# One 512-column matmul for the high weight block in three projections, with the two halves added by VectorE

## The reference, cut to what matters

```
q    = xt @ w_pq                      # layer 1, 2048 x 2048, then q . sub_k1, q . sub_k2, top-k, experts
xBC  = proj[:, 4096:10240]            # layer 2, h @ in_w, 6144 of its columns
xBC  = silu(causal_depthwise_conv(xBC, conv_w, conv_b))   # 4 taps along the tokens
k, v = split(x @ kv_w, 2, axis=-1)    # layer 3, k is 2048 x 3072
```

## Time and profile before

| | |
|---|---|
| time, median of 3 (us) | 3421.45 (3420.68 to 3424.72) |
| span of the profiled execution (us) | 3418.1 |
| PE, DVE, ACT, POOL busy | 95%, 70%, 47%, 19% |
| chain that ended last: PE, DVE, issue, ACT | 83%, 5%, 3%, 3% |

### The profile page before, as it was taken

How to read it: one execution, slowest core, us unless ns; L and a number is a source line. 1 busy time by engine, 2 the same in 40 slices (tenths; PEclk the granted TensorE clock), 3 DMA queues, 4 the chain that set the end, 5 groups by cost and what they waited for, 6 DMA issues and landing times.

```text
span 3418.1 us, 64505 instructions
## 1 busy us (share of the span) xinstructions
PE 3259.0 (95%) x21980; PEld 2977.2 (87%) x21980; DVE 2395.3 (70%) x3845; ACT 1602.5 (47%) x2243; POOL 661.4 (19%) x635
## 2 busy tenths in 40 slices
PE   7999999999999999999999989999999999999997
PEld 7787899999889998899777879998888779987996
DVE  6675459189778987799898776335888877554455
ACT  4654446533454344433344555545665444444442
POOL 1000029800111001100000116885221111100000
PEclk9999999999999999999999999999999999999998
DMA  6434544666787668866555874666665886765443
GB/s 195 148 99 140 162 148 153 186 203 212 235 264 225 211 211 258 263 201 213 167 172 177 265 245 123 185 190 191 208 208 172 272 267 220 248 194 177 136 131 140
DMA packets 185651, 667.86 MB, mean 195 GB/s; under 512 B 24160, under 2 KB 24384, under 8 KB 184368
## 3 DMA queue, kind: packets, MB, share of 16 engines
q1 hardware_dynamic: 149696, 545.91, 50.1%
q0 software_dynamic: 35824, 120.19, 11.0%
HBM read 663.83 MB, written 2.18 MB: 195 GB/s over the span
## 4 chain that ended last, share of the span: by engine, by line
PE 83%; DVE 5%; issue 3%; ACT 3%; PEld 2%; POOL 2%; DMA 1%; DVEq 0%; POOLq 0%; PEldq 0%; ACTq 0%; SPq 0%
PE PS L556 14%; PE PS L557 14%; PE PS L558 14%; PE PS L881 7%; PE PS L883 7%; PE PS L885 7%; PE PS L627 2%; PE PS L628 2%; PE PS L629 2%; POOL w_lo L473 2%; PE PS L1058 2%; PE PS L1060 2%; PE PS L1062 2%; PE PS L833 1%; ACT w_hi L1222 1%
## 5 line engine op out<-in xcount | busy, mean ns | idle before, releaser
L1222 ACT ACTIVATE w_hi<-raw 128x1024 fp32r<-128x1024 f32 x1032 | 1092.7, 1060 | 1627.4 <-PE PS L558 925.1
L1717 DVE TENSOR_TENSOR w_lo<-raw,w_hi 128x1024 fp32r<-128x1024 f32 x872 | 1065.1, 1224 | 650.0 <-ACT w_hi L1222 642.7
L556 PE MATMUL PS<-xt_hi,w_hi 128*128 128x256 f32 x4608 | 1332.1, 289 | 22.4 <-POOL w_lo L473 6.6
L557 PE MATMUL PS<-xt_lo,w_hi 128*128 128x256 f32 x4608 | 1312.0, 285 | 0.0
L558 PE MATMUL PS<-xt_hi,w_lo 128*128 128x256 f32 x4608 | 1311.1, 285 | 0.0
L556 PEld LDWEIGHTS PS<-xt_hi,w_hi 128*128 128x128 f32 x4608 | 891.8, 194 | 34.1 <-issue 23.8
L557 PEld LDWEIGHTS PS<-xt_lo,w_hi 128*128 128x128 f32 x4608 | 892.3, 194 | 0.4
L558 PEld LDWEIGHTS PS<-xt_hi,w_lo 128*128 128x128 f32 x4608 | 891.7, 194 | 0.0
L473 POOL TENSOR_TENSOR w_lo<-raw,w_hi 128x1024 fp32r<-128x1024 f32 x160 | 404.7, 2538 | 222.4 <-ACT w_hi L1222 221.4
L881 PE MATMUL PS<-w_hi,st_hi 128*128 128x512 f32 x1024 | 403.1, 394 | 1.5 <-issue 1.3
L883 PE MATMUL PS<-w_hi,st_lo 128*128 128x512 f32 x1024 | 399.9, 391 | 0.0
(11 more groups left out here) (387 smaller groups left out, 3573.6 us busy)
## 6 DMA issues: line engine op xcount, KB each, us to landing
raw<-in_u_emb SPq DMA_DIRECT2D x256, 512.0 KB, 3.7
raw<-in_v_emb SPq DMA_DIRECT2D x256, 512.0 KB, 4.4
ada<-in_ada_w POOLq DMA_DIRECT2D x240, 256.0 KB, 4.3
raw<-in_xbc SPq DMA_DIRECT2D x96, 512.0 KB, 3.6
raw<-in_z SPq DMA_DIRECT2D x80, 512.0 KB, 3.7
raw<-in_q SPq DMA_DIRECT2D x64, 512.0 KB, 3.6
raw<-in_a_out SPq DMA_DIRECT2D x64, 512.0 KB, 4.3
raw<-in_k SPq DMA_DIRECT2D x48, 512.0 KB, 4.2
```

The lines of the kernel that those rows point to most:

```text
L556: pe.matmul(o, w_h, x_h, start=start, stop=False, skip_group_check=True)
L557: pe.matmul(o, w_h, x_l, start=False, stop=False, skip_group_check=True)
L1222: act.activation(w_hi[:, u, :], raw[:, u, :], ACT.Copy).then_inc(hi_done, 1)
L1717: dve.tensor_tensor(w_lo[:, u, :], raw[:, u, :], w_hi[:, u, :].bitcast(F32), ALU.subtract)\
```

## The change

`xt_hi` and `xt_lo` become the two halves of one tensor `xt`. In w_pq, xbc and k2 the first two of the three matmuls become one of 512 columns: the high weight block by `xt_hi` (to columns 0 to 255 of the bank) and by `xt_lo` (to columns 256 to 511). The low weight block by `xt_hi` adds to columns 0 to 255. The two halves of the bank are then added by a tensor_reduce on DVE in all three stages; ACT takes out nothing in them any more. In xbc the sum goes to `xtmp` in SBUF, the bank is freed at once, and the convolution reads `xtmp`.

```diff
-        xt_hi = sb("xt_hi", [P, KC, S], F32R)
-        xt_lo = sb("xt_lo", [P, KC, S], F32R)
+        xt = sb("xt", [P, 2, KC, S], F32R)
+        xt_hi, xt_lo = xt[:, 0, :, :], xt[:, 1, :, :]
...
+            def halves(o, w_h, w_l, k, start, stop):
+
+                pe.matmul(o.rearrange("p (a s) -> p a s", a=2), w_h, xt[:, :, k, :], start=start, stop=False,
+                          skip_group_check=True)
+                return pe.matmul(o[:, 0:S], w_l, xt_hi[:, k, :], start=False, stop=stop, skip_group_check=True)
+
+            def wide_product(name, j, b):
+
+                for h in range(2):
+                    u = 2 * b + h
+                    pe.wait_ge(lo_done, 4 * j + (4 * FIRST_BODY[name] + u + 1))
+                    for k in range(8):
+                        w = slice(k * P, k * P + P)
+                        last = halves(PS[:, b, :], w_hi[:, u, w], w_lo[:, u, w], 8 * h + k,
+                                      h == 0 and k == 0, h == 1 and k == 7)
+                    last.then_inc(tile_used, 1)
...
-            turned_blocks("w_pq", act_free, ACT_BLOCKS["w_pq"], 1)
+            turned_wide("w_pq", DVE_BLOCKS["w_pq"], 1)
...
-            bodies("w_pq", lambda i, b: act.activation(
-                one(pqT, i), PS[:, b, 0:S], ACT.Copy).then_inc(act_free, 1))
+            bodies("w_pq")
...
+            def added_halves(o, b):
+
+                return dve.tensor_reduce(o, PS[:, b, :].rearrange("p (a s) -> p s a", a=2), AX.X, ALU.add)
+
+            def query_out(i, b):
+
+                added_halves(one(pqT, i), b).then_inc(dve_free, 1)
...
                     dve.wait_ge(tile_used, 4 * j + (4 * FIRST_BODY["xbc"] + 2 * b + 2))
+                    link(added_halves(xtmp[:, b, :], b))
+                    dve.sem_inc(dve_free, 1)
                     dve.wait_ge(sem("conv_read"), i + 1)
-                    convolve(cbuf[:, b, :], PS[:, b, 0:S], lambda t: pc[:, ds(4 * i + (PC["a_conv_w"] + t), 1)], 3)
-                    dve.sem_inc(dve_free, 1)
+                    convolve(cbuf[:, b, :], xtmp[:, b, :], lambda t: pc[:, ds(4 * i + (PC["a_conv_w"] + t), 1)], 3)
                     dve.sem_inc(sem("conv_done"), 1)
...
                         low(j + FIRST_BODY[name] + 1, u)
+                        if name == "k2" and u % 2 == 1:
+                            dve.wait_ge(tile_used, 4 * j + (4 * FIRST_BODY["k2"] + u + 1))
+                            added_halves(one(k2T, 2 * j + u // 2), u // 2).then_inc(dve_free, 1)
                         if u:
                             ada_product("kv2", j + first_k, u - 1, ada_k, ada_acc_k)
```

More of the change, by code:

```diff
@@ L355, in build @@
         act_free, dve_free = sem("act_free"), sem("dve_free")
-        ACT_BLOCKS = {"gate": 0, "w_pq": 8, "up0": 24, "up1": 56, "up2": 88, "up3": 120, "z": 152, "k2": 184, "q2": 208}
-        DVE_BLOCKS = {"rec": 0, "xbc": 8}
+        ACT_BLOCKS = {"gate": 0, "up0": 8, "up1": 40, "up2": 72, "up3": 104, "z": 136, "q2": 168}
+        DVE_BLOCKS = {"rec": 0, "w_pq": 8, "xbc": 24, "k2": 72}
         CHUNKS = {"down0": 0, "down1": 64, "down2": 128, "down3": 192, "a_out": 256}
@@ L577, in channel_blocks, with turned_wide @@
                         block_product(name, j, b, PS[:, b, 0:S])
+            def turned_wide(name, before, n, between=()):
+                for h in range(2):
+                    pe.wait_ge(lo_done, 4 * FIRST_BODY[name] + h + 1)
+                    for k in range(8):
+                        pe.wait_ge(xt_lo_done, KC * n + max(8 * h + k, 8) + 1)
+                        w = slice(k * P, k * P + P)
+                        last = halves(PS[:, 0, :], w_hi[:, h, w], w_lo[:, h, w], 8 * h + k,
+                                      h == 0 and k == 0, h == 1 and k == 7)
+                    last.then_inc(tile_used, 1)
+                pe.wait_ge(dve_free, before + 2)
+                wide_product(name, 0, 1)
+                start = 1
+                for end, work in (*between, (NB[name], None)):
+                    if end > start:
+                        with pe.Fori(start, end) as j:
+                            for b in range(2):
+                                pe.wait_ge(dve_free, 2 * j + before + b + 1)
+                                wide_product(name, j, b)
+                    if work:
+                        work()
+                    start = end
             def turned_blocks(name, free, before, n, between=()):
@@ L797, in _ @@
             turn(1, lambda tt: diag[:, tt, :])
-            turned_blocks("w_pq", act_free, ACT_BLOCKS["w_pq"], 1)
+            turned_wide("w_pq", DVE_BLOCKS["w_pq"], 1)
             pe.wait_ge(sem("keys_loaded"), 16)
-            pe.wait_ge(act_free, 2 + ACT_BLOCKS["w_pq"] + 16)
+            pe.wait_ge(dve_free, 2 + DVE_BLOCKS["w_pq"] + 16)
             for tt in range(TT):
@@ L1003, in first_group @@
                 cb_group(0)
-            turned_blocks("xbc", dve_free, DVE_BLOCKS["xbc"], 2,
-                          ((1, step_and_modulation), (6, turn_steps), (22, first_group)))
+            turned_wide("xbc", DVE_BLOCKS["xbc"], 2, ((1, step_and_modulation), (6, turn_steps), (22, first_group)))
             pe.wait_ge(sem("mod_done"), 7)
@@ L1092, in _ @@
             turn(3)
-            turned_blocks("k2", act_free, ACT_BLOCKS["k2"], 3)
+            turned_wide("k2", DVE_BLOCKS["k2"], 3)
             ada_sum("a_out", 3, ada_acc_a)
-            pe.wait_ge(act_free, 2 + ACT_BLOCKS["k2"] + 24)
+            pe.wait_ge(dve_free, 2 + DVE_BLOCKS["k2"] + 24)
             def turn_shifted(c):
@@ L1622, in _ @@
             balanced(3, pc[:, PC["ln_g"]:PC["ln_g"] + KC], pc[:, PC["ln_b"]:PC["ln_b"] + KC], normed_columns)
-            bodies("k2", lambda i, b: act.activation(
-                one(k2T, i), PS[:, b, 0:S], ACT.Copy).then_inc(act_free, 1))
+            bodies("k2")
             f = FIRST_BODY["v2"]
@@ L2003, in _ @@
             turned(1, lambda c: pc[:, PC["g_ffn"] + c:PC["g_ffn"] + c + 1])
-            bodies("w_pq")
+            def added_halves(o, b):
+                return dve.tensor_reduce(o, PS[:, b, :].rearrange("p (a s) -> p s a", a=2), AX.X, ALU.add)
+            def query_out(i, b):
+                added_halves(one(pqT, i), b).then_inc(dve_free, 1)
+            query_out.links = 0
+            bodies("w_pq", query_out)
             def best(values, left, o_values, o_indices, n):
@@ L2283, in _ @@
             with dve.Fori(6, 22) as j:
-                link.loop_from(j, 6, 8)
+                link.loop_from(j, 6, 10)
                 convolved_body(j)
@@ L2309, in _ @@
             with dve.Fori(22, NB["xbc"]) as j:
-                link.loop_from(j, 22, 8)
+                link.loop_from(j, 22, 10)
                 convolved_body(j)
```

## The result

| | before | changed |
|---|---|---|
| time, median (us) | 3421.8 (3420.68 to 3424.72, 4 runs) | 3495.58 (3492.25 to 3498.3, 4 runs) |
| ratio | | 1.0215 (1.0202 to 1.0228) |
| span of the profiled execution (us) | 3418.1 | 3496.6 |

The changed kernel is 2.15% slower, 74 us, where the forecast had 30 us slower and a range up to 3480. The loss is in one stage. Its bounds here are two places that both kernels have: PE's first matmul of the turn of `X` (`diag` by `X`) ahead of xbc starts at 2042.09 before and 2043.21 after, and the modulation sum in the next stage, z, at 2627.61 and 2707.65. Between them lie 585.5 us before and 664.4 us after, +78.9 us. The rest of the span together is about as long as before.

The account below looks back on a forecast made before the run. PE, busy 95% of the span, was taken as the bound, with DVE becoming it in xbc. w_pq -1.8, k2 -3.3 and xbc +35 gave +30 us, 3451 us; range 3427 to 3480.

Parts of the forecast that it names:

- What PE gains: All three stages: one matmul's fixed 13.3 ns saved per slice, 346.7 instead of 360 ns; 18.8 us if PE stays the bound.
- The reduction: DVE's tensor_reduce of 512 elements from PSUM takes 0.72 us; it reads only PSUM and isn't held.
- w_pq: Stage w_pq: PE gains 3.4 us, the last reduction delays the scores by 1.6; sum -1.8 us.
- k2: Stage k2: PE gains 5.1 us, bank waits cost 1.1 and the end 0.6; sum about -3.3 us.
- xbc, the holding: In xbc, DVE operations reading SBUF alone wait for the running POOL subtraction: 2.5 us instead of 0.58, 1.9 more.
- xbc, the size: DVE's steady body in xbc: 12.7 us, chosen between 11.1 and 14.1, over PE's 11.1; xbc in all +35 us.
- the upper bound, 14.1: DVE's body in xbc if each of POOL's four subtractions holds one operation: 6.5 + 7.6 = 14.1 us.
- Bodies 1 to 3: First xbc bodies, where DVE also does the softplus, 34 of 34.6 us full: 0 to 12 us more, taken as 7.
- steady price: Each of 24 xbc bodies takes 12.7 instead of 11.5 us: +28 us.
- Sum: Whole kernel: -1.8 - 3.3 + 35 = +30 us, median 3451 us.
- the third rival: In xbc every subtraction holds DVE, or pauses lower PE's clock: 14.1 us a body, +69, 3491 us; chance 0.08.
- the fourth rival: The two strips cost as much as two matmuls; w_pq and k2 lose their 8.5 us: 3460 us; chance 0.04.

Follow-up runs that it names:

- experiment 1: Changed kernel, but in xbc the halves are added into PSUM bank 5 or 6 and the convolution reads that: 3417.78 us, ratio 0.9989.
- experiment 2: Kernel before, but in xbc DVE copies the block from PSUM to xtmp, frees the bank and convolves from xtmp: 3484.6 us, ratio 1.0187.
- experiment 6: Changed kernel, but DVE instead of POOL makes w_lo in xbc: 3465.83 us, ratio 1.0127.
- experiment 8: Changed kernel, xtmp still in SBUF, but the convolution accumulates in PSUM bank 5 or 6 and the SiLU reads that: 3415.17 us, ratio 0.9982.
- experiment 9: Changed kernel, but POOL makes each w_lo of xbc in two subtractions of 512 columns instead of one of 1024: 3450.29 us, ratio 1.008.

## Why the prediction was wrong

The mechanism, its place and the direction were right, the size was not, and the time fell out of the range. By the prediction's own steps:

- **What PE gains** (-18.8 us if PE stays the bound). The columns and the fixed 13.3 ns per matmul were read rightly, but a pair has two distances, 346.7 and 353.3 ns, so the gain per slice is 13.3 or 6.7 ns. No row of the kernel before shows the second. Two strips cost nothing that the runs show: one strip has the same two distances.
- **The reduction** was forecast at 0.72 us and takes 0.69, and it is never held. Right.
- **w_pq** (-1.8 us): the end costs the 1.6 us, the gain is 1.7; sum 0.0. **k2** (-3.3 us): the waits are 0.4 for a bank and 0.3 at the end, in place of 1.1 and 0.6. From k2's turn to the first matmul of the next stage, v2, are 151.35 us, 1.9 less than before; v2 itself is 1.2 longer, at a granted clock of 0.95 where it had 0.97.
- **xbc, the holding.** Right for the operations that it priced: held to the end of POOL's instruction, 2.46 us for a held operation (forecast 2.5), one operation for each subtraction, DVE the bound (experiments 1, 2, 6, 8 and 9). Its rule, "a DVE operation that reads SBUF alone waits", was too wide: the tensor_scalar of experiment 8 reads `xtmp` and isn't held.
- **xbc, the size: the step that failed.** "Between them I choose by what is likely to lie beside POOL without being held: the two reductions, 1.4 us. That gives 12.7 us." Measured: 15.13 us. 1.4 of the missing 2.4 us are that choice: SiLU, high part and subtraction follow the end of a convolution, so the reduction is over when the subtractions begin. It was to be seen before: the text itself names the SiLU ahead of the high parts, but uses it only for how the loop closes, and not for where the subtractions fall. The other 1.0 us are in the main the pauses about the reduction: 0.15 us a block for its semaphores were put in, 0.6 to 0.9 are there (0.37 and 0.22 or 0.51 in the timeline), 1.15 us a body more. So the upper bound, 14.1, was no bound either. The whole body by its rows: reductions 1.38, tensor_scalar 0.70, scalar_tensor_tensor 11.30, pauses 1.75, together 15.13 us.
- **Bodies 1 to 3** (+7 beside the steady price). From the first tensor_scalar of xbc to that of block 8 the changed kernel falls 6 us behind, about what the forecast's steady price of 1.2 us makes for these four bodies; the 7 on top did not come. The sum took DVE as full there, 34 of 34.6 us, but these four bodies take 62.8 us in the kernel before (2059.03 to 2121.87), and not 46. From block 8 to block 47 DVE falls back another 70 us, 3.6 a body.
- **Sum.** What came is the third rival, "held by every subtraction" (3491 us, 0.08), within 5 us. Its chance was too low and the range left it out. That it is so near is in part luck: its body was 1.0 us too short, and its 12 us for bodies 1 to 3 didn't come. The range's upper end, 3480, is also not the middle that the text names: the forecast and the fourth rival (3460) would give 3455, the forecast and the third 3471.

## What to carry to other kernels

Before an operand moves from PSUM to SBUF, count the SBUF inputs of each VectorE operation that reads it, and look at what GpSimd runs at that time: with two of them (or a tensor_scalar from SBUF to SBUF), each of GpSimd's subtractions here could hold one for its whole length, and leaving the source or the accumulator in PSUM took all of that away (experiments 1 and 8). When one engine can hold another, don't discount by chance overlap: follow what releases each of them. Here the loop closed on one phase, and of the two orders that were run it was the worse one. With the holding gone, the change itself is worth 0.1 to 0.3% (0.9989, 0.9982 and, with one strip, 0.9972), which is not clearly more than w_pq and k2 alone give (0.9984).

## What was not expected of the hardware

Back-to-back pairs of a wide and a narrow matmul run at one of two distances, 346.7 or 353.3 ns, at the full granted clock, and the same code shows either in the same stage in different executions. In the stretches of the kernel before that were read the earlier trace rows, matmuls of 256 columns alone show 120.0 ns and those of 512 alone 226.7. Over 1408 pairs the difference is up to 9.4 us. Whether it makes the scatter of the times is not shown: ten runs of experiment 8 lie between 3408.15 and 3420.87 us, but the kernel before, which has no such pairs, scatters nearly as much in the same session, 3418.55 to 3427.82. The value changed after a wait of PE in k2. What sets it stays open.
